# One hybrid encoder layer on one Trainium2 core: where VectorE computes the next round's output maps in the S5 branch

## The reference

```python
proj = h @ w_in                              # z | xBC | dt | u_s5 | gate_a, gate_b
y_a = _ssd_branch(z, xbc, dt_raw, ...)       # conv, chunked scan in both directions, RMSNorm, w_out
y_b = _s5_branch(u, ...)                     # below
mix = sigmoid(g_a) * y_a + sigmoid(g_b) * y_b
h = _layer_norm(ALPHA * h + mix @ w_o, ...)
h = _layer_norm(ALPHA * h + _expert_choice_ffn(h, ...), ...)   # 16 experts, FF 2816

def _s5_branch(u, ...):                      # 48 groups of 16 channels, 64 complex states each
    s_f = states of x_k = Abar x_{k-1} + Bbar u_k      # forward in time
    s_b = the same, backward in time
    y = real(einsum(s_f + s_b, c)) + u * d_skip
    y = gelu(y)
    return (y @ w_glu_a) * sigmoid(y @ w_glu_b)
```

## Time and profile before

| | |
|---|---|
| median of 3 runs | 2244.28 us (2242.2 to 2245.69) |
| the profiled execution | 2238.59 us, its span 2236.8 us |
| PE busy | 1989.3 us (89%) |
| DVE busy | 685.0 us (31%) |
| ACT busy | 335.2 us (15%) |
| POOL busy | 317.1 us (14%) |
| HBM traffic | 614.39 MB read |

### The profile page before, as it was taken

How to read it: one execution, slowest core, us unless ns; L and a number is a source line. 1 busy time by engine, 2 the same in 40 slices (tenths; PEclk the granted TensorE clock), 3 DMA queues, 4 the chain that set the end, 5 groups by cost and what they waited for, 6 DMA issues and landing times.

```text
span 2236.8 us, 19826 instructions
## 1 busy us (share of the span) xinstructions
PE 1989.3 (89%) x8350; PEld 937.8 (42%) x8350; DVE 685.0 (31%) x1114; ACT 335.2 (15%) x553; POOL 317.1 (14%) x282
## 2 busy tenths in 40 slices
PE   9886899998988999799989879889989888988987
PEld 4544454455554444444334334334334333333332
DVE  6599974579972113500000000000000000000002
ACT  1332312234452002100000000000001000000001
POOL 1866610056660000000000000000000000000001
PEclk9898899999998999899999999989989999999999
DMA  5621222101112227489999999999999999999995
GB/s 139 123 80 49 69 65 75 66 29 43 39 60 104 85 94 318 190 365 425 428 428 424 430 427 426 428 428 427 428 427 426 429 426 427 428 428 427 428 426 223
DMA packets 86921, 625.47 MB, mean 280 GB/s; under 512 B 21052, under 2 KB 34608, under 8 KB 57648
## 3 DMA queue, kind: packets, MB, share of 16 engines
q1 hardware_dynamic: 74400, 616.41, 67.3%
q10 hardware_dynamic: 12432, 7.79, 1.1%
HBM read 614.39 MB, written 9.78 MB: 279 GB/s over the span
## 4 chain that ended last, share of the span: by engine, by line
PE 47%; DMA 29%; DVE 10%; ACT 2%; issue 1%; SPq 0%; DVEq 0%; ACTq 0%
PE ps L881 46%; DMA arena<-in_w_e 29%; DVE arena L1689 1%; ACT arena L594 1%; DVE arena L1637 1%; DVE arena L1693 1%; DVE arena L1664 1%; DVE arena L1694 1%; ACT L594 1%; DVE arena L1662 1%; DVE arena L1690 0%; DVE arena L1681 0%; DVE arena L1766 0%; DVE arena L1764 0%; DVE arena L1686 0%
## 5 line engine op out<-in xcount | busy, mean ns | idle before, releaser
L881 PE MATMUL ps<-arena 128*64 128x512 f32 (+8 forms) x7818 | 1925.1, 532 | 218.7 <-DMA arena<-in_w_e 104.6
L881 PEld LDWEIGHTS ps<-arena 128*64 128x64 f32 (+2 forms) x7818 | 877.7, 164 | 1247.2 <-issue 1052.9
L594 ACT ACTIVATE arena<-ps 128x512 f32<-128x512 f32 (+4 forms) x286 | 160.8, 595 | 1635.7 <-PE ps L881 908.3
L1823 DVE TENSOR_TENSOR arena<-arena,ps 128x512 f32<-128x512 f32 (+1 forms) x48 | 30.2, 644 | 577.2 <-PE ps L881 577.2
L586 POOL TENSOR_TENSOR arena<-arena 128x1024 f32<-128x1024 f32 x3 | 7.0, 2348 | 1371.8 <-ACT arena L594 1371.8
L1832 DVE TENSOR_TENSOR arena<-arena,ps 128x512 f32<-128x512 f32 x48 | 33.1, 690 | 331.8 <-PE ps L881 331.8
L594 ACT ACT_TABLE_LOAD x77 | 98.8, 1283 | 24.2 <-issue 22.1
L594 ACT ACTIVATE arena<-arena 64x512 f32<-64x512 f32 (+6 forms) x138 | 62.9, 513 | 207.2 <-DVE arena L1694 95.3
L1622 DVE SCALAR_TENSOR_TENSOR arena<-arena 128x512 f32<-128x512 f32 x80 | 62.5, 781 | 2.8
L1814 DVE TENSOR_TENSOR arena<-arena 128x512 f32<-128x512 f32 x8 | 5.6, 694 | 184.6 <-PE ps L1350 184.6
L567 POOL TENSOR_TENSOR arena<-arena 128x768 f32<-128x768 f32 x16 | 24.4, 1524 | 171.4 <-PE ps L1046 134.1
(11 more groups left out here) (191 smaller groups left out, 761.9 us busy)
## 6 DMA issues: line engine op xcount, KB each, us to landing
arena<-in_w_e SPq DMA_DIRECT2D x128, 2816.0 KB, 29.0
arena<-in_w_e SPq DMA_DIRECT2D x80, 2048.0 KB, 28.5
arena<-in_w_in SPq DMA_DIRECT2D x9, 2048.0 KB, 8.6
arena<-in_w_e SPq DMA_DIRECT2D x16, 1024.0 KB, 31.5
arena<-in_w_in SPq DMA_DIRECT2D x5, 1536.0 KB, 6.4
arena<-in_w_out_ssd SPq DMA_DIRECT2D x4, 1536.0 KB, 6.7
gate_scratch<-arena ACTq DMA_DIRECT2D x16, 256.0 KB, 2.4
arena<-gate_scratch SPq DMA_DIRECT2D x4, 1024.0 KB, 8.0
```

The costliest lines, as they stand in the source:

```text
L594: return act.activation(out, in_, func, **kw)
L881: return pe.matmul(out, lhsT, rhs, start=a, stop=z)
L1823: tt(o, o, ps[:, i, 0:w], ALU.mult).then_inc(s.hid_ready, 1)
```

## The change

In each round VectorE used to compute the maps of the next round first, then the Toeplitz rows, then both recurrences. Now it takes the Toeplitz rows and the forward recurrence first, then the next round's maps, then the backward recurrence. No instruction is added, removed or reshaped, the other engines' lists are untouched, and the number of maps, six, is the same.

```diff
             for q in range(NQ):
-                if q + 1 < NQ:
-                    maps(q + 1)
                 if q == 0:
                     dve.wait_ge(s.seg_exp, 1)
                     n.done(tt(w_end, w_end, dtime, ALU.mult))
                 toeplitz_rows(q)
-                for d in range(2):
-                    recur(q, d)
+                recur(q, 0)
+                if q + 1 < NQ:
+                    maps(q + 1)
+                recur(q, 1)
```

## The result

The changed kernel takes 2277.13 us (median of 5 runs, 2274.14 to 2278.0) against 2244.28 us before in the same session: ratio 1.0146, 95% interval [1.0128, 1.0163], so 29 to 37 us slower. The forecast was 2277. The profiled execution took 2277.82 us, its span is 2276.1 us.

The account below looks back on a forecast made before the run. VectorE's rounds bound the kernel up to the handover at 286.96 us, TensorE from there. The terms put the handover 32.4 us later: 2238.59 becomes 2271, and with 5.7 for the median 2277; range 2261 to 2293.

Parts of the forecast that it names:

- Step 1: `maps(1)` leaves an idle stretch ahead of round 0 for a place between its recurrences, where nothing is idle: +10.4 us.
- Step 2: Forward recurrence of round 0 takes 16.2 us, from 98.43 to 114.6, with GpSimd through its start-up 2.5 us sooner.
- Step 3: End of maps to F: 16.7 us, 31.2 in round 1; VectorE idles some 5.4 us a round, about 20 in round 1.
- Step 4: Rounds after round 1: forward recurrence 14.8 us, period 41.9 us against 38.9 before, the last maps ending at 302.7.
- M(2) to M(3): One period from the end of `maps(2)` to the end of `maps(3)`, claimed as 41.9 us.
- Step 5: TensorE's `outputs(4)`, behind `states(5)`, can start only at F(5), 319.4 instead of 286.96: +32.4 us in sum.
- M(1): End of `maps(1)` in round 0, claimed at 125.0 us.
- B: Round trip from the second maps on 11.3 us or less, no idle: round 39.9 us, +20.1, median 2264; chance 0.13.
- C: GpSimd and VectorE take turns: maps beside tables 12.1 us, about +16 us more in all, median 2293; chance 0.11.
- D: Not slower: less contention, F always there, round 32.8 us, handover 20 us earlier, median 2224; chance 0.03.

Follow-up runs that it names:

- Two rounds ahead: Changed kernel with `maps(1)` ahead of round 0 and `maps(q + 2)` between the recurrences of round q: 2254.3 us, ratio 1.0057 to the kernel before.
- the gates first: Changed kernel with ScalarE copying each round's gates ahead of `block_diagonal` of the next round: 2261.0 us, ratio 1.0082 to the kernel before.
- the last round only: Kernel before with only `maps(5)` moved between the recurrences of round 4: 2255.47 us, ratio 1.0058.
- both edits: Changed kernel with `maps(1)` ahead of round 0 and ScalarE's gates ahead of the next `block_diagonal`: 2259.75 us, ratio 1.0082 to the kernel before.
- no tables: GpSimd's tables of rounds 1 to 5 left out, in two kernels: the kernel before, 2222.73 us, and the changed kernel, 2240.04 us.

## Why the prediction was right

*Step 1, `maps(1)` loses its cover:* right. The block takes 10.78 us in the new place (10.4 forecast), the wait ahead of L1599 grew to 16.85 us (near 19 forecast), and putting the block back is worth 9 us.

*Step 2, `recur(0, 0)`:* 16.4 us (16.2 forecast). GpSimd ended the tables of round 0 at 106.73, 3.7 us after F(0), against 6.2 before: the 2.5 us that were estimated.

*Step 3, the round trip:* right in path and size. ScalarE waits for the maps and not for GpSimd, and TensorE for ScalarE. Rows of the changed kernel, ScalarE in round 1, TensorE in rounds 0 and 1:

```profile
182.29 5.24 ACT L594 ACTIVATE arena<-arena 64x512 f32<-64x512 f32 x12 [16.07 <-DVE arena L1432]
```

```profile
137.38 17.68 PE L881 MATMUL ps<-arena 128*128 128x512 f32 x64 [20.70 <-ACT arena L594]
...
189.58 3.59 PE L881 MATMUL ps<-arena 128*32 128x64 f32 x32 [10.27 <-ACT arena L594]
```

From the end of the maps to F it is 31.0 us in round 1 (31.2 forecast), then 17.8, 17.5, 17.1 and 16.7 (16.7 forecast). The excess of the first ones goes with TensorE's clock. Windows of TensorE alone (busy, granted clock, DMA share, GB/s): `toeplitz(2)` and the transposes behind it, then those transposes in round 5:

```profile
189.50:193.10 3.60, 3.52 (x32) 0.50 0.21 77
193.10:195.80 2.70, 2.70 (x14) 0.54 0.35 118
...
318.86:321.20 2.34, 2.09 (x19) 1.00 0.39 135
```

In round 2, behind 10.27 us idle, TensorE ran at 1.2 GHz (granted 0.50) in `toeplitz`, as in the earlier trace rows, and at 0.54, mostly 1.2 GHz, in the first transposes too; I had counted the former only. In rounds 3 and 4 the granted clock in those transposes was 0.76 and 0.96, in round 5 1.00, and the trips shorten with it.

*Step 4, the later rounds:* the forward recurrences took 13.6, 13.8 and 14.0 us (14.8 forecast), since F came a little later and the wait covered more of `state_maps`. That the two errors, one too long and one too short, cancel is luck, and the period is 42.2 us where M(2) to M(3) is taken (41.9 forecast).

*Step 5, the handover:* right. F(5), 16.7 us behind the maps; `outputs(4)` directly behind `states(5)`. The sum was +32.4, the traces give +33.5, the medians +32.9. The trace is 0.6 us over the forecast by M(1), 0.3 by the slightly longer maps of round 1, 0.3 in the three periods, and 0.2 under it in the trip of round 1. So the mechanism and its terms held within a few us; that the median, 2277.13, fell on the forecast's 2277 is luck as well, since the traces compared are single executions, and the 5.7 us added to make a median came from three runs. The end moved by 1.2 us more than the handover, which the forecast had as equal.

The rivals: B (F on time) would have needed the waits to be absent; "Two rounds ahead" nearly is that kernel in rounds 2 and 3, with a round of 40.6 us where B had 39.9. C (GpSimd and VectorE take turns wholly, the strict reading of the Trainium skill's rule in "SBUF — State Buffer", section "SBUF: two separate sides") gave 12.1 us for maps beside tables; the trace has 10.78, so it does not bear the strict reading out. D fell with the first wait. It was right that contention would fall (23 us less of VectorE's busy time) and wrong that it could outweigh the waits.

## What to carry to other kernels

When one block of a busy engine's list is moved later, count from the block's end what other engines still have to do before that engine needs the result: here 17 us stood behind the maps, cover went from 26 to 10, and a move without a single instruction more cost 1.5%. The first round is a case of its own, because a block that once ran in the start-up's idle time has no such place in the loop. And the same reorder of a helping engine can help in one order and hurt in the other, so it has to be followed to the handover.

## What the runs showed of the hardware

The rows can be read so that the slow-down beside GpSimd goes by instruction more than by bytes. VectorE in the backward recurrence of round 1 of the kernel before, a combination and a scan beside table instructions of GpSimd, and a later scan alone:

```profile
159.04 1.33 DVE L1576 TENSOR_TENSOR arena<-arena 128x512 f32<-128x512 f32 x1
...
163.19 1.42 DVE L1582 TENSOR_TENSOR_SCAN arena<-arena 128x128 f32<-128x128 f32 x1
...
164.84 0.40 DVE L1582 TENSOR_TENSOR_SCAN arena<-arena 128x128 f32<-128x128 f32 x1
```

A 128-element scan goes from 0.40 to 1.42 us, and the 512-element combination from 0.69 to 1.33 (the earlier trace rows has the 0.69). GpSimd's table instructions beside them took 1.38 to 1.59 us, and about one of them went by for each instruction of VectorE. Beside the 256-element instructions of `state_maps` a scan took 0.84. In these rows the short VectorE instruction lost the larger factor, 3.6 against 1.9. No run here varied the size of the instructions by itself, so this is a reading of the rows and not tested.

The stages behind the handover do not always take the same time, though their lists of instructions are the same. From the handover to the start of the 144.47 us piece it is 419.7 us before (286.96 to 706.67) and 419.8 after the change (325.01 to 744.84), and between 419.2 and 420.0 in three other runs; in the six with the gates first, two rounds ahead, the last round only, both edits and no tables (two) it is 423.3 to 424.6. Part of it lies in the SSD scan. Its window in the kernel with the last round alone:

```profile
482.50:644.40 161.90, 143.71 (x536) 89.30 (x535) 147.42 (x192) 69.52 (x98) 99.81 (x58) 0.95 0.09 30
```

161.9 us at a granted 0.95, and 161.9 at 0.96 with the gates first, against 159.1 at 0.98 before and 158.9 at 0.96 after, so not a plain function of the mean clock; the cause stays open. Where medians and handovers disagree by 2 to 5 us here, this is one place that it can come from, and the fast execution of before is another.
